# Two-block network on one core: the second mixer's scan gets its cumulated decays as rows, spread by 32-deep products, and walks head group by head group

## What is computed

```python
a_cum = jnp.cumsum(dt_c * A.reshape(G, R), axis=2)
seg = a_cum[:, :, :, None] - a_cum[:, :, None, :]
decay = jnp.exp(jnp.where(lower, seg, -jnp.inf))
cb = jnp.einsum('bcign,bcjgn->bcijg', Cc, Bc)
y_diag = jnp.einsum('bcijg,bcijgr,bcjgrp->bcigrp', cb, decay, xdt)
...
y_off = jnp.einsum('bcign,bcigr,cbgrpn->bcigrp', Cc, jnp.exp(a_cum), h_in)
y = (y_diag + y_off).reshape(b, l, H, P).astype(xh.dtype)
```

## Time and profile before

| | |
|---|---|
| Times of three runs | 3516.07, 3516.30, 3517.92 us; median 3516.3 |
| Span of the profiled execution | 3517.1 us (its whole time is one of the three; the profile gives the span) |
| PE busy | 3333.0 us, 95% of the span |
| DVE, ACT, POOL busy | 1738.0, 673.3, 302.6 us |
| Second mixer's scan, from the first L1570 to the end of `outputs(15)` | 2471.5 to about 2649.4 us |
| One scan step, n < 8 | 11.7 us |

### The profile page before, as it was taken

How to read it: one execution, slowest core, us unless ns; L and a number is a source line. 1 busy time by engine, 2 the same in 40 slices (tenths; PEclk the granted TensorE clock), 3 DMA queues, 4 the chain that set the end, 5 groups by cost and what they waited for, 6 DMA issues and landing times. The chain is left out here.

```text
span 3517.1 us, 39734 instructions
## 1 busy us (share of the span) xinstructions
PE 3333.0 (95%) x15231; PEld 2389.2 (68%) x15231; DVE 1738.0 (49%) x2533; ACT 673.3 (19%) x1097; POOL 302.6 (9%) x238
## 2 busy tenths in 40 slices
PE   6999998999999999999899999899989998899998
PEld 5888854488887888855478887555765887434342
DVE  4665457366646666348276644524336655211122
ACT  1111015111101111013221100531553101100001
POOL 2111000111100111000101100100330000000000
PEclk9999998999999999999899999999999999999999
DMA  5443221334322433222224321322113232899996
GB/s 134 117 104 102 80 60 36 84 90 117 95 82 84 115 94 101 91 56 60 70 74 114 94 90 48 92 72 84 43 30 90 84 108 100 355 409 409 410 410 267
DMA packets 469520, 453.36 MB, mean 129 GB/s; under 512 B 33867, under 2 KB 418174, under 8 KB 469149
## 3 DMA queue, kind: packets, MB, share of 16 engines
q1 hardware_dynamic: 467312, 449.97, 39.8%
q10 hardware_dynamic: 1452, 1.67, 0.4%
q0 software_dynamic: 640, 0.15, 0.0%
HBM read 445.96 MB, written 5.77 MB: 128 GB/s over the span
## 5 line engine op out<-in xcount | busy, mean ns | idle before, releaser
L465 PE MATMUL psum<-arena 128*128 128x256 f32 x7392 | 1616.2, 380 | 2.3 <-DVE arena L814 2.3
L465 PEld LDWEIGHTS psum<-arena 128*128 128x128 f32 x7392 | 1398.9, 190 | 203.9 <-issue 7.0
L879 DVE TENSOR_TENSOR arena<-arena 128x512 f32<-128x512 f32 (+2 forms) x152 | 96.4, 634 | 602.7 <-PE psum L465 573.6
L2360 PE MATMUL psum<-arena 128*64 128x512 f32 x1536 | 345.8, 600 | 1.6 <-ACT arena L2457 1.6
L354 POOL TENSOR_TENSOR arena<-arena 128x1024 f32<-128x1024 f32 x96 | 180.9, 1906 | 1037.6 <-DVE arena L869 993.0
L2360 PEld LDWEIGHTS psum<-arena 128*64 128x64 f32 x1536 | 104.8, 137 | 235.5 <-issue 228.4
L703 ACT COPY arena<-psum 128x256 f32<-128x256 f32 x104 | 38.9, 374 | 1177.1 <-PE psum L465 1177.0
L1677 PE MATMUL psum<-arena 128*128 128x256 f32 x1120 | 243.0, 379 | 1.4 <-DVE arena L2082 1.4
L1677 PEld LDWEIGHTS psum<-arena 128*128 128x128 f32 x1120 | 211.7, 189 | 32.6 <-DVE arena L2082 1.8
L575 PE MATMUL psum<-arena 128*128 128x512 f32 x416 | 183.1, 595 | 10.0 <-DVE arena L1021 6.3
L869 DVE TENSOR_REDUCE arena<-arena 128x256 f32<-128x2048 f32 x48 | 177.5, 3698 | 0.0
(11 more groups left out here) (422 smaller groups left out, 3011.9 us busy)
## 6 DMA issues: line engine op xcount, KB each, us to landing
arena<-in_w_gate_dram SPq DMA_DIRECT2D x64, 1024.0 KB, 14.0
arena<-in_w_up_dram SPq DMA_DIRECT2D x64, 1024.0 KB, 15.0
arena<-in_w_down_dram SPq DMA_DIRECT2D x64, 1024.0 KB, 17.4
arena<-in_ffn_w_gate_dram SPq DMA_DIRECT2D x88, 512.0 KB, 6.2
arena<-in_ffn_w_up_dram SPq DMA_DIRECT2D x88, 512.0 KB, 7.2
arena<-in_ffn_w_down_dram SPq DMA_DIRECT2D x96, 384.0 KB, 3.7
arena<-in_w_in_dram SPq DMA_DIRECT2D x144, 256.0 KB, 3.2
arena<-in_ada_w_dram SPq DMA_DIRECT2D x48, 512.0 KB, 4.0
```

The lines of the kernel that those rows point to most:

```text
L465: mm = pe.matmul(psum[:, b0 + b, c:c + HT], w, right(x), start=(first and c == 0), stop=last, skip_group_check=True)
L879: dve.tensor_tensor(sv[:, 0, :, :], a21, a22, ALU.add)
L2360: mm = pe.matmul(psum[64 * e:64 * e + 64, bank0 + half, :], x[:, k, 64 * e:64 * e + 64], ring[u % SLOTS][:, e, half * 512:(half + 1) * 512 ...
```

## The change

Each step's 8 products from broadcast columns go away. In their place, once, between the `LAT1` units and `to_tokens`, `cumulated_rows` makes 32 products with 32-column weights: for every group, way and chunk t, the 4 heads' decays of chunk t (padded with zeros to 32 columns, `dta_pad`) against the triangular matrix, written to partitions 32t to 32t+31. A head's cumulated decays are then a row. ACT copies the two banks to SBUF (`cum_rows`). For each group DVE multiplies them with a 0/1 column `own_row` into `spread_rows` (128 x 1024), which holds head h's row in column block h of the same partition, and zeros elsewhere. A step then needs two products, 32 deep (partitions 32c to 32c+31) and 512 wide, with ones as weights. The steps walk all chunks of a group before the next group, so that there are 4 spreads in all. The pad is zeroed by POOL, and filled by 4 small copies on DVE behind `time_steps`.

```diff
         ws_in = place(8, 128)
+        own_row = place(4)
+        dta_pad = cb.rearrange("p s h i -> p (s h i)").rearrange("p (g w t c) -> p g w t c", g=4, w=2, t=4)
+        rows_at = wsum_at + 2048
+        cum_rows = [arena[:, at:at + 512].rearrange("p (g w i) -> p g w i", g=2, w=2)
+                    for at in (wsum_at + 704, rows_at)]
+        spread_rows = arena[:, rows_at + 768:rows_at + 1792].rearrange("p (w h i) -> p w h i", w=2, h=4)
+        assert rows_at + 1792 <= xm_at
...
-        names = ("ctx_in small_in wdt_in ones_ok pads_ok consts ctx_tr ctx_t a_exp "
+        names = ("pad_zero pad_ok rows_done rows_ok spread_ok ctx_in small_in wdt_in ones_ok pads_ok consts ctx_tr ctx_t a_exp "
                  "unit_done sqc_ready varc_done zero_ok stdc_ready nc_ready xmc_ready sql_act sql_dve varl_done "
...
             pool.sem_inc(s["consts"], 1)
+            pool.wait_ge(s["varc_done"], 1)
+            pool.memset(cb, 0.0).then_inc(s["pad_zero"], 1)
             for n in range(NT * G):
-                c, g, b = n // G, n % G, n % 2
+                g, c, b = n // NT, n % NT, n % 2
                 ct = xbc[:, CM + g, c * CH:(c + 1) * CH].unsqueeze(1).to_broadcast([128, 4, CH])
...
                 mm.then_inc(s["cum_done"], 1)
+            def cumulated_rows():
+                pe.wait_ge(s["pad_ok"], 1)
+                pe.wait_ge(s["ac_ready"], 1)
+                for g in range(G):
+                    for way, tri in ((0, tri_f), (1, tri_b)):
+                        at = (g % 2) * 256 + way * CH
+                        for t in range(NT):
+                            mm = pe.matmul(psum[32 * t:32 * t + 32, 4 + g // 2, at:at + CH], dta_pad[:, g, way, t, :],
+                                           tri, start=True, stop=True)
+                mm.then_inc(s["rows_done"], 1)
...
             units(LAT1, 2, xm, T)
+            cumulated_rows()
             to_tokens(xbc_c, NC, 0, 4 + 12)
...
-                c, g, b = n // G, n % G, n % 2
+                g, c, b = n // NT, n % NT, n % 2
+                if c == 0:
+                    pe.wait_ge(s["spread_ok"], g + 1)
                 if n >= 2:
...
                           start=True, stop=True)
-                for way, tri in ((0, tri_f), (1, tri_b)):
-                    for h in range(4):
-                        col = dta[:, c, H * way + 4 * g + h:H * way + 4 * g + h + 1]
-                        mm = pe.matmul(psum[:, 2 + 3 * b + way, h * CH:(h + 1) * CH],
-                                       col.to_broadcast([128, 128]), tri, start=True, stop=True)
+                own = slice(32 * c, 32 * c + 32)
+                for way in range(2):
+                    mm = pe.matmul(bank(2 + 3 * b + way), ones1[own, :],
+                                   spread_rows[own, way, :, :].rearrange("p h i -> p (h i)"), start=True, stop=True)
                 mm.then_inc(s["bc_done"], 1)
...
             def outputs(n):
-                c, g, b = n // G, n % G, n % 2
+                g, c, b = n // NT, n % NT, n % 2
                 pe.wait_ge(s["cc_ready"], n + 1)
...
             scan_units(LAT1, 2, pad_l, T, xbc, 4)
+            act.wait_ge(s["rows_done"], 1)
+            for j in range(2):
+                last = act.copy(cum_rows[j].rearrange("p g w i -> p (g w i)"), bank(4 + j))
+            last.then_inc(s["rows_ok"], 1)
             token_copies(NC, 0)
...
             dve.tensor_reduce(same_head, ident.rearrange("p (g h) -> p h g", h=32), AX.X, ALU.add)
+            dve.tensor_reduce(own_row, ident.rearrange("p (g h) -> p h g", h=32)[:, 0:4, :], AX.X, ALU.add)
             dve.sem_inc(s["zero_ok"], 1)
...
             time_steps(1, 0, NT + NC)
+            dve.wait_ge(s["pad_zero"], 1)
+            dve.drain()
+            for t in range(NT):
+                last = dve.tensor_copy(dta_pad[:, :, :, t, 0:4],
+                                       dta[:, t, :].rearrange("p (w g h) -> p g w h", w=2, g=4))
+            last.then_inc(s["pad_ok"], 1)
             scan_units(CTX + 1, 5, pad_c, C, 2)
...
+            def spread(g):
+                if g:
+                    dve.wait_ge(s["bc_done"], NT * g)
+                else:
+                    dve.wait_ge(s["rows_ok"], 1)
+                dve.tensor_tensor(spread_rows, cum_rows[g // 2][:, g % 2, :, :].unsqueeze(2).to_broadcast([128, 2, 4, CH]),
+                                  own_row.unsqueeze(1).unsqueeze(3).to_broadcast([128, 2, 4, CH]), ALU.mult)\
+                   .then_inc(s["spread_ok"], 1)
             def combine(n):
-                c, g, b = n // G, n % G, n % 2
+                g, c, b = n // NT, n % NT, n % 2
                 m = df[:, b, :, :]
...
+            spread(0)
             masked(0)
...
                 combine(n)
+                if n % NT == 2 and n // NT + 1 < G:
+                    spread(n // NT + 1)
             skip(NT * G - 1)
```

## The result

The changed kernel takes 3546.2 us (median of 4 runs, 3542.94 to 3547.57) against 3516.24 us (3516.07 to 3517.92): a ratio of 1.008, 95% interval [1.0066, 1.0095]. It is 30 us slower. The forecast was no change: 3520.2 us, in a range from 3513 to 3527.

The account below looks back on a forecast made before the run. PE, busy 95% of the span, was taken to set the pace. Steps, first spread, row copies and pads summed to +4.75 us; the clock added -2.6 and +1.7, giving +3.85 us: 3520.2 us, range 3513 to 3527.

Parts of the forecast that it names:

- Step 7, the clock: Granted clock: the fall in `to_tokens` goes, -2.6 us; a fall comes at the scan's start, +1.7 us.
- Step 1, the products: Two 512-wide products for eight in each scan step on PE: +0.13 us a paced step, together +1.8 us (-1.1 to +3.5).
- Step 3, the first spread: On DVE between the last `pass_state` and `bcasts(0)`, without cover: +1.2 us.
- Steps 2, 4, 5: Three later spreads on DVE, hidden, 0; rows on PE, 3.5 us, hidden, 0; row copies on ACT, +1.05 us.
- Step 6, the pads: Four pad copies on DVE behind `time_steps`, holding the next convolutions, ACT and PE: +0.7 us (0.6 to 1.4).
- Step 7, the transposes: First transposes in `to_tokens`: PE idles only some 1.3 us, so the clock fall there goes, -2.6 us.
- The one-time parts together: Ahead of the scan: first spread +1.2, row copies +1.05, pad copies +0.7, saved clock fall -2.6 us.
- Rival A: Two depth switches a scan step, 0.42 us each for empty array and uncovered weight load: +15.5 us, 3531.8; chance 0.10.
- Rival B: Clock: no fall saved in `to_tokens`, one at the scan's start, one more in last steps: +8.2 us, 3524.5; chance 0.22.

Follow-up runs that it names:

- x1: Changed kernel with each step's two spread products 128 deep, weights with ones in the chunk's 32 rows and zeros elsewhere; 3522.05 us, ratio 1.001.
- x9: Changed kernel, 32 deep, with the next step's C.B and both spread products moved behind the first v half or unit products, covering the wait; 3518.51 us.
- x5: Changed kernel with the two spread products 64 deep, using the half of the partitions where the chunk's rows lie; 3532.71 us, ratio 1.0042.
- x8: Changed kernel, still 32 deep, with the second spread product moved a quarter into the v half or unit in steps 1 to 12; 3534.96 us.
- x2: Changed kernel with each 32-deep product 512 wide cut into four 128 wide, sixteen passes a step; 3547.74 us, ratio 1.0079.
- x10: Kernel before, with only the next step's products moved behind the first v half or unit products, covering the wait for `skip`; 3507.97 us, ratio 0.9971.

## Why the prediction was wrong, point by point

- **Step 7, the clock, failed.** It looked for falls where PE idles, and took a PE that streams 32-deep products for a PE at work. In the paced steps it had no term at all, which put the clock there at nothing without a reason. There the clock fell behind 0.79 us of waiting and 1.9 us of shallow products, at 1.7 us a fall: 13.71 us a step, against 12.04 for the 64-deep step without one. Eleven steps make 18 of the 27 us. Full depth (x1) takes it away, and so does covering the wait (x9). The trace of the kernel before had a warning: in `cumulate`, 36 full-depth passes that stream 16 or 32 columns, PE is busy all the time, without an idle time since 2299.88, and the clock falls (stretches of 1 us, as above):

```profile
2309.00:2310.00 1.00, 1.00 (x11) 1.00 (x10) 0.29 (x1) 0.79 (x2) 0.00 (x0) 1.00 1.13 341
2310.00:2311.00 1.00, 1.00 (x7) 1.00 (x8) 0.00 (x0) 0.98 (x2) 0.00 (x0) 0.57 0.28 81
```

- **Step 1, the products**, had the right mechanism and too small a size. The two changes of depth cost 0.32 us a step (x5), where I took the middle, 0.13; 0.35 by x8. My upper value of 0.22 had both gaps counted as real, which they are: from C.B to the v half it takes 2.30 us, 0.21 more than before, and the v half itself starts slowly, 7.20 in place of 7.10 in x5. Over 11 steps this is 3.5 us, not 1.4. The slow first pass is of the kind of the drain that the Trainium skill names for a change of tiling mode ("TensorEngine Tiling", Key Properties), and the 0.32 us are about three times my estimate from its pages. What the traces show is the weight load that starts with its product and no longer ahead of it (x5).
- **Step 3, the first spread**: 1.23 us as said, PE's wait 3.67 (3.5 said). The fall at the scan's start came, and cost more than 1.7 us: the clock stayed down through both `bcasts` and into the v half. With the changes of depth, and without the spread, which lies ahead of it, that stretch took 5.25 us more. At full depth the same idle time left a fall too (2.62 and 2.68 us for the first two lots of spread products in x1), a shorter one: 1.25 us more (15.28 against 14.03).
- **Steps 2, 4, 5**: right. The three later spreads took 1.54 us each beside POOL, and nobody waited for them. The rows took 1.97 us, not 3.5: their pace is 0.031 us a pass against 0.112 for full width, as if nearly four went at a time. They go to four different quarters of the output partitions in turn; the passes of L1426 that I had read stand at 0.061 us. Row copies 1.05 us as said.
- **Step 6, the pads**: 0.45 us for the four copies (0.7 said); PE's wait grew from 5.08 to 5.27 us.
- **Step 7, the transposes**: half right. The block behind took 27.78 us, at full clock throughout as I had it, but the clock still fell, earlier: 0.86 in the same 12 us, and the transposes stayed slow (3.58 us for 16).
- **The one-time parts together** came out near the forecast: up to the first C.B product steps 3, 5, 6 and the saved fall add to +0.35 us, and +0.17 was measured. Part of this is luck: PE stood 0.56 us ahead at 2270 us already, before it had run anything of the change (2270.14 and 2269.58, starts of the same unit). Counted from there it is +0.73 us.
- **Rival A** gave the right side by a mechanism that is there (a change of depth does cost, and its weight load isn't covered) but is far too small: it had 0.42 us a switch, where 0.16 were measured, some 5 us over 16 steps. Its mark, "a step of 12.2 us or more would make A right", was met by 13.7 us and did not tell it from the clock; a sign that names a step time without the clock beside it proves little. The rule of the Trainium skill on weight loads and row groups ("TensorE: Matmul & The Clock Gate", Part 3), which I set beside it, didn't show: four 32-deep passes take 1.98 us from first start to last end, 0.1 more than full-depth ones in x1 (1.89).
- **Rival B** had the clock as the cause, in the wrong place (ahead of the scan and in its last steps) and at a quarter of the size, 8.2 us of 30.

What stays open: how the fall depends on depth between 32 and 128, and on where the wait and the shallow stretch lie in time. 64 deep fell in the first steps and then not; 32 deep fell in every paced step of the changed kernel, but not in three of the last four in x2. The runs show the ends, not the law.

## What to carry to other kernels

A busy PE isn't enough to hold its clock. Here four passes that used 32 of the 128 rows took 1.98 us, full ones 1.89, and a short wait and this shallow stretch, each harmless alone, brought a fall in most steps where they stood next to each other; the price was paid by the full-depth work behind. Where a shallow product saves no passes, try it at full depth with zeros (here 24 us). Before adding anything behind a small wait in a loop, cover the wait: here that alone gave 10 us.

## What I had not expected of the hardware

- The clock level at a busy PE: 1.00 with full-depth products, 0.87 with 32-deep ones in one seventh of the step, at nearly the same busy share (0.93, 0.94) and behind the same wait of 0.79 us.
- Zeros count: with 96 zero rows of 128 in the weights, the clock stays at 1.00 in the paced steps (x1).
- 64 passes with 32-column weights in 1.97 us, 0.03 us each, against 0.112 us for passes of full width.
- A change between full and shallow depth and back costs 0.32 us (x5) to 0.35 us (x8), also where no wait is near: a step takes 11.20 us in x9 and 10.88 in x10.
